# Two transformer blocks in one kernel: order of the opening, of the delta rule's decays and of two smaller steps

## The reference, cut to what matters

```python
h = rmsnorm(x, norm_mix_g);  proj = h @ w_in          # 1024 x 9248: qkv, z, gates ga and gb, ...
qkv = silu(causal_depthwise_conv(concat([gq, gk, gv]), gdn_conv_w))       # 3 x 8 heads x 128
g = -exp(a_log) * softplus(ga + dt_bias);  beta = sigmoid(gb)
# gated delta rule, chunk by chunk; gc = cumsum(g) within a chunk
decay = exp(where(incl, gc[:, None] - gc[None, :], -inf))
lower = where(strict, beta[:, None] * (k @ k.T) * decay, 0)
u, w  = triangular_solve(lower, [beta * v, beta * exp(gc) * k], unit_diagonal=True)
a_qk  = (q @ k.T) * decay
delta = u - w @ state;  o = (q * exp(gc)) @ state + a_qk @ delta
state = exp(gc[-1]) * state + (k * exp(gc[-1] - gc)).T @ delta
o_a = rmsnorm(o) * silu(z)                                     # z: one of w_in's parts
# gated linear attention, 4 heads: scores of decayed q and k, then the same recurrence
# second block: mod = silu(c) @ ada_w + ada_b (for tokens), mod_c the same of c_ctx
```

## Time and profile before

| | us |
|---|---|
| median of three executions | 2690.18 |
| lowest, highest | 2688.42, 2690.37 |
| the profiled execution: time | 2693.22 |
| the profiled execution: span from first to last instruction | 2691.6 |
| busy in it: PE, DVE, ACT, POOL | 2604.5, 1388.5, 908.1, 160.8 |
| granted TensorE clock, mean over the span | 0.987 |

### The profile page before, as it was taken

One profiled execution on the slowest core, in us unless ns is written; L12 is line 12 of the kernel. 1 busy time (PEld: TensorE's weight loads), 2 busy tenths in 40 slices (PEclk: granted clock), 3 DMA queues, 4 the chain that ended last, 5 costly groups with the idle time before them and its releaser, 6 DMA issues.

```text
span 2691.6 us, 34182 instructions
## 1 busy us (share of the span) xinstructions
PE 2604.5 (97%) x14939; PEld 2188.7 (81%) x14939; DVE 1388.5 (52%) x1679; ACT 908.1 (34%) x1254; POOL 160.8 (6%) x177
## 2 busy tenths in 40 slices
PE   6998999999999999999999989899999999999998
PEld 5887888888889788888888977778888788788887
DVE  5665544344466347665565177376643544443334
ACT  4342223343334442222432267332222322322222
POOL 0003110000000010000022000100000100000001
PEclk9999999999999999999999999999999999999999
DMA  3220002221334234563222100166522222222321
GB/s 124 93 79 18 27 8 79 94 79 63 107 112 144 77 125 172 184 210 124 93 87 79 63 1 1 63 221 217 194 103 86 86 98 100 85 94 95 109 91 67
DMA packets 39301, 265.73 MB, mean 99 GB/s; under 512 B 4256, under 2 KB 4640, under 8 KB 8944
## 3 DMA queue, kind: packets, MB, share of 16 engines
q1 hardware_dynamic: 29520, 205.67, 22.1%
q0 software_dynamic: 8256, 55.41, 5.9%
q10 hardware_dynamic: 1376, 2.47, 0.2%
HBM read 261.43 MB, written 2.10 MB: 98 GB/s over the span
## 4 chain that ended last, share of the span: by engine, by line
PE 88%; DVE 7%; ACT 4%; issue 1%; DMA 0%; DVEq 0%; ACTq 0%
PE bank L142 87%; DVE w_lo L151 1%; ACT w_hi L148 1%; PE bank L145 1%; DVE tmp L159 1%; DVE dd L151 1%; ACT da_p L148 1%; DVE da_stat L162 1%; DVE h_lo L159 0%; ACT L148 0%; ACT tmp L148 0%; DVE heads_t L159 0%; ACT da_pt L148 0%; DVE change L151 0%; DVE x_t L159 0%
## 5 line engine op out<-in xcount | busy, mean ns | idle before, releaser
L142 PE MATMUL bank<-h_hi,w_hi 128*128 128x512 f32 (+1 forms) x1992 | 797.7, 400 | 12.8 <-DVE w_lo L151 9.1
L142 PE MATMUL bank<-h_hi,w_lo 128*128 128x512 f32 (+1 forms) x1992 | 780.5, 392 | 0.0
L142 PE MATMUL bank<-h_lo,w_hi 128*128 128x512 f32 (+1 forms) x1992 | 746.2, 392 | 3.9 <-DVE h_lo L151 3.8
L151 DVE TENSOR_TENSOR w_lo<-w_raw,w_hi 128x2048 fp32r<-128x2048 f32 (+2 forms) x197 | 444.9, 2259 | 308.1 <-ACT w_hi L148 308.0
L148 ACT ACTIVATE w_hi<-w_raw 128x2048 fp32r<-128x2048 f32 (+2 forms) x197 | 370.6, 1881 | 311.0 <-PE bank L142 301.2
L142 PEld LDWEIGHTS bank<-h_hi,w_hi 128*128 128x128 f32 (+1 forms) x1992 | 376.0, 189 | 94.7 <-DVE w_lo L151 11.3
L142 PEld LDWEIGHTS bank<-h_lo,w_hi 128*128 128x128 f32 (+1 forms) x1992 | 374.9, 188 | 90.2 <-DVE h_lo L151 10.2
L142 PEld LDWEIGHTS bank<-h_hi,w_lo 128*128 128x128 f32 (+1 forms) x1992 | 376.3, 189 | 74.7 <-issue 1.4
L142 PE MATMUL bank<-f_hi,w_hi 128*128 128x512 f32 x672 | 263.0, 391 | 0.0
L142 PE MATMUL bank<-f_hi,w_lo 128*128 128x512 f32 x672 | 262.4, 390 | 0.0
L142 PE MATMUL bank<-f_lo,w_hi 128*128 128x512 f32 x672 | 248.7, 390 | 0.0
(11 more groups left out here) (332 smaller groups left out, 3241.1 us busy)
## 6 DMA issues: line engine op xcount, KB each, us to landing
w_raw<-in_pack_ffn SPq DMA_DIRECT2D x60, 1024.0 KB, 4.9
ada_w<-in_ada_w POOLq DMA_DIRECT2D x48, 1024.0 KB, 5.3
w_raw<-in_pack_mlp SPq DMA_DIRECT2D x32, 1024.0 KB, 5.1
w_raw<-in_pack_gdn_qkv SPq DMA_DIRECT2D x12, 1024.0 KB, 4.9
w_raw<-in_pack_sc_cu SPq DMA_DIRECT2D x8, 1024.0 KB, 4.9
w_raw<-in_pack_ffn SPq DMA_DIRECT2D x8, 768.0 KB, 4.2
w_raw<-in_pack_gdn_z SPq DMA_DIRECT2D x4, 1024.0 KB, 4.9
w_raw<-in_pack_gate_a SPq DMA_DIRECT2D x4, 1024.0 KB, 5.0
```

What stands on the lines that cost most here:

```text
L142: return self.engine.matmul(*a, **k) if self.engine is not None else self
L151: return self.engine.tensor_tensor(*a) if self.engine is not None else self
```

## The change

1. **Opening.** The parts of `x` are the first DMAs: parts 1 and 3 on ScalarE's queue ahead of `prm`, parts 0 and 2 on SyncE's ahead of panel 0; SyncE holds panel 1 back until part 1 of `x` has landed; `kept_consts` and `scan_consts` go to GpSimd's queue. The waits for constants stand behind the squares. `gates_tensor` does panel 1 (the first two tiles of q) in the same loop over k as the gates; panel 1's hi x lo follows behind the loop, and the splits of panels 1 and 2 move up. TensorE gets five extra matmuls of 384 columns on constants (`warm_up`).
2. **Delta rule.** The decays of chunk c+1 are computed behind level 8 of chunk c, its products k k^T and `low` behind `p64`, its first level behind `change`; those of chunk 0 before z's GEMM. The decays lie in `e_t`, `e_row` for even chunks and in `tmp` for odd ones, decay times beta in `sq`. z's panels are split in four pieces of 512 columns.
3. **Gated linear attention.** A head's scores come one step of the background later (9 yields for 8, and one fewer behind them).
4. **Modulation.** A yield between the sums of `ada_acc` and of `ada_accc`; ScalarE, VectorE and GpSimd have one to match.

```diff
+    def split_hi_piece(S, n, i):
+
+        cut = slice(i * panel_size(n) // PIECES, (i + 1) * panel_size(n) // PIECES)
+        if i == 0:
+            S.wait_ge(*loaded(f"raw_loaded{n % 2}", n // 2 + 1))
+            S.wait_ge(*at("pe_tile", ("panel", n - 2)))
+        S.activation(w_hi[n % 2][:, cut], w_raw[n % 2][:, cut], ACT.Copy).then_inc(
+            *up("act_hi", (n, i), *([n] if i == PIECES - 1 else [])))
...
+    def gemm_beside(lane, split, key, evacuate, block=0, panels=None, token_tiles=0, split_from=0,
+                    piece=None):
 
         for i, nk, width, groups, first in panel_groups(key, block, panels, token_tiles):
-            if split is not None and i >= split_from:
-                split(lane, number[key, block, i] + 1)
+            ahead = number[key, block, i] + 1
+            if split is not None and i >= split_from and piece is None:
+                split(lane, ahead)
+            steps = 0
             for group in groups:
                 for k in range(nk):
+                    if piece is not None and steps < 2 * PIECES and steps % 2 == 0:
+                        piece(lane, ahead, steps // 2)
+                    steps += 1
                     yield
...
+    def load_x(lane, parts):
+        for i in parts:
+            lane.dma_start(x_t[:, 2 * i:2 * i + 2, :], x_in[:, 2 * i:2 * i + 2, :]).then_inc(sems[f"x_loaded{i}"], 16)
+
     def load_scalar(S):
+        load_x(S, (1, 3))
         S.dma_start(prm[:, :], dram["params"]).then_inc(sems["prm_loaded"], 16)
-        S.dma_start(kept_consts[:, :, :], consts_in[:, 0:N_KEPT, :]).then_inc(sems["consts_loaded"], 16)
-        for i in range(DT // 2):
-            S.dma_start(x_t[:, 2 * i:2 * i + 2, :], x_in[:, 2 * i:2 * i + 2, :]).then_inc(sems[f"x_loaded{i}"], 16)
+
+    def load_pool(G):
+        G.dma_start(kept_consts[:, :, :], consts_in[:, 0:N_KEPT, :]).then_inc(sems["consts_loaded"], 16)
+        G.wait_ge(*loaded("x_loaded3"))
+        G.dma_start(scan_consts[:, :, :], consts_in[:, N_KEPT:, :]).then_inc(sems["scan_consts_loaded"], 16)
...
+    def warm_up(T_, rings, name, n):
+
+        bank, before = rings.work.take(("busy", name))
+        T_.wait_ge(*freed(before))
+        T_.wait_ge(*loaded("consts_loaded"))
+        for _ in range(n):
+            done = T_.matmul(bank[:, 0:N_KEPT * P], const("ident"), flat(kept_consts[:, :, :]), start=True, stop=True)
...
+        T_.wait_ge(*at("act_hi", 1))
         for k in range(DT):
             rounded, rest = mix_norm.done(k)
             T_.wait_ge(*rounded)
-            T_.matmul(bank[0:32, :], hi[:, k, :], h_hi[:, k, :], start=(k == 0), stop=False)
-            T_.matmul(bank[0:32, :], lo[:, k, :], h_hi[:, k, :], start=False, stop=False)
+            T_.matmul(g_out, g_hi[:, k, :], h_hi[:, k, :], start=(k == 0), stop=False)
+            T_.matmul(g_out, g_lo[:, k, :], h_hi[:, k, :], start=False, stop=False)
+            for out, cut in q_outs:
+                T_.matmul(out[:, :], q_hi[:, k, cut], h_hi[:, k, :], start=(k == 0), stop=False)
             T_.wait_ge(*rest)
-            done = T_.matmul(bank[0:32, :], hi[:, k, :], h_lo[:, k, :], start=False, stop=(k == DT - 1))
-        done.then_inc(*up("pe_tile", tile, ("panel", 0)))
+            done = T_.matmul(g_out, g_hi[:, k, :], h_lo[:, k, :], start=False, stop=(k == DT - 1))
+            if k == DT - 1:
+                done.then_inc(*up("pe_tile", gates, ("panel", 0)))
+            for out, cut in q_outs:
+                T_.matmul(out[:, :], q_hi[:, k, cut], h_lo[:, k, :], start=False, stop=False)
+        T_.wait_ge(*at("dve_lo", 1))
+        for tile, (out, cut) in zip(queries, q_outs):
+            for k in range(DT):
+                done = T_.matmul(out[:, :], q_lo[:, k, cut], h_hi[:, k, :], start=False, stop=(k == DT - 1))
...
     def gates_scalar(S):
-        split_hi(S, 1)
+        split_hi(S, 2)
...
+    def decays_of(grp, c):
+
+        if c % 2:
+            return four_heads(tmp[grp]), four_heads(tmp[2 + grp])
+        return scan_tiles[grp]["e_t"][:, :, :], scan_tiles[grp]["e_row"][:, :, :]
...
+        def decays(c):
+            bank = bank_for(c, "e_row")
+            four(bank, lambda h: gv[:, c, 4 * grp + h:4 * grp + h + 1].to_broadcast([P, P]),
+                 lambda h: const("incl_t")).then_inc(*up("pe_gdn", (grp, c, "e_row")))
+
+        def products(c):
+            k_of = lambda h: k_t[:, 4 * grp + h, chunk_of(c)]
+            bank = bank_for(c, "low")
+            four(bank, k_of, k_of).then_inc(*up("pe_gdn", (grp, c, "low")))
...
+                if s == 8 and c < NCH - 1:
+                    yield
+                    decays(c + 1)
...
+                yield
+                products(c + 1)
...
     def scan_scalar(S, grp):
...
+        def decays(c):
+            e_t, e_row = (flat(a) for a in decays_of(grp, c))
+            S.wait_ge(*at("dve_gdn", (grp, c, "between")))
+            S.activation(e_t, e_t, ACT.Exp).then_inc(*up("act_gdn", (grp, c, "e_t")))
+            if c >= 2:
+                S.wait_ge(*at("pool_gdn", (grp, c - 2, "q_decayed")))
+                S.wait_ge(*at(state_by(c - 2), (grp, c - 2, "state")))
+            take(c, "e_row", e_row, whole, ACT.Exp)
...
+                if s == 8 and c < NCH - 1:
+                    yield
+                    decays(c + 1)
...
+        def products(c):
+            e_t, _ = decays_of(grp, c)
+            V.wait_ge(*at("act_gdn", (grp, c, "e_t")))
+            V.tensor_tensor(e_beta, e_t, col_of(bv3, c), ALU.mult).then_inc(*up("dve_gdn", (grp, c, "e_beta")))
+            bank = psum(c, "low")
+            V.wait_ge(*at("dve_gdn", (grp, c, "e_beta")))
             if c > 0:
-                V.wait_ge(*at("pe_gdn", (grp, c - 1, "state")))
-            V.tensor_tensor(change[:, :, :], e_t[:, :, :], col_of(bv3, c), ALU.mult).then_inc(
-                *up("dve_gdn", mark("e_beta")))
-            bank = psum(c, "low")
-            V.wait_ge(*at("dve_gdn", mark("e_beta")))
+                V.wait_ge(*at("pool_gdn", (grp, c - 1, f"off{LEVELS[-1]}")))
             for i, half in enumerate(HALVES):
-                V.tensor_tensor(low[half, :, :], change[half, :, half], bank4(bank)[half, :, half], ALU.mult).then_inc(
-                    *up("dve_gdn", mark(f"low{i}")))
-            yield
-            V.wait_ge(*at("dve_gdn", mark("low1")))
+                V.tensor_tensor(low[half, :, :], e_beta[half, :, half], bank4(bank)[half, :, half], ALU.mult).then_inc(
+                    *up("dve_gdn", (grp, c, f"low{i}")))
             if c > 0:
-                V.wait_ge(*at("pe_gdn", (grp, c - 1, "state")))
+                V.wait_ge(*at("pe_gdn", (grp, c - 1, "p64")))
+            V.tensor_tensor(corner[0:HB, :, :], e_beta[0:HB, :, HB:P], bank4(bank)[0:HB, :, HB:P],
+                            ALU.mult).then_inc(*up("dve_gdn", (grp, c, "corner"), frees=(grp, c, "low")))
...
+            if c < NCH - 1:
+                first_level(c + 1)
...
     def scan_with_gate_tensor(T_, rings):
         rings.gemm, wide = rings.few, rings.gemm
         steps = in_turn([scan_tensor(T_, rings, 0), scan_tensor(T_, rings, 1)])
+        for _ in range(4):
+            next(steps)
         drain(beside(z_tensor(T_, rings, "gdn_z"), steps, *SCAN_PACE))
         drain(steps)
...
-            for _ in range(8):
+            for _ in range(9):
                 yield
...
                 done.then_inc(*up("pe_ada", (layer, j, which)))
-            yield
+                yield
...
     def tensor_program(T_):
         rings = Rings()
         Ring.holder.clear()
-        constants_there(T_)
+        warm_up(T_, rings, "sums", 3)
         mix_sum.over_partitions(T_, rings)
         mix_sum.spread(T_, rings)
+        warm_up(T_, rings, "first", 2)
         gates_tensor(T_, rings)
...
+            if n == 0:
+                load_x(Y, (0, 2))
+            elif n == 1:
+                Y.wait_ge(*loaded("x_loaded1"))
+            else:
                 Y.wait_ge(*at("dve_lo", n - 2))
```

More of the change, by code:

```diff
@@ L930, in conv_tensor @@
         T_.background, T_.pace = scan_sums_tensor(T_, rings), 4
-        drain(gemm_tensor(T_, rings, "gdn_qkv", h_done(mix_norm), after=squares))
+        for _ in range(2):
+            T_.step()
+        drain(gemm_tensor(T_, rings, "gdn_qkv", h_done(mix_norm), panels=(1, 12), after=lambda n: squares(n + 2)))
         T_.finish()
@@ L1283, in scan_vector @@
+        products(0)
+        first_level(0)
+        yield
+        for c in range(NCH):
+            mark = lambda name: (grp, c, name)
+            a_t, e_row = decays_of(grp, c)
+            yield
             bank = psum(c, "a_t")
-            V.tensor_tensor(flat(a_t[:, :, :]), flat(e_t[:, :, :]), bank[:, :], ALU.mult).then_inc(
+            V.tensor_tensor(flat(a_t), flat(a_t), bank[:, :], ALU.mult).then_inc(
                 *up("dve_gdn", mark("a_t"), frees=mark("a_t")))
@@ L1389, in scan_pool @@
                     off_level(c, 4 * s)
-            for _ in range(4 + 2 * (c < NCH - 1)):
```

(11 more changed lines are left out.)

148 lines of the change are left out of this document (80 added, 68 removed).

## The result

The changed kernel takes 2669.03 us (median of four, 2667.59 to 2671.17), the kernel before 2690.27: ratio 0.9929, 95% interval 0.9914 to 0.9944. It is 21 us faster; I had forecast 35 (2655). The whole range, 2641 to 2671, just holds it, but my own case's, 2647 to 2661, does not. The direction was right and the size was not.

A forecast was written before the change was run, and what follows sets the result against it. TensorE, busy 2604.5 of 2691.6 us, was taken to bound the kernel, leaving idle time and half clock to gain: opening 8.5, delta rule 15.9, linear attention 7.6, modulation 3.4, sum 35.4; forecast 2655 us, range 2641 to 2671.

The forecast's parts named there:

- my own case: Whole kernel: all four parts gain as summed, 2655 us, range 2647 to 2661, chance 0.6.
- Apart by an output tile, 24 matmuls: Modulation: separating the sums of one column avoids the half clock behind them; gain 3.4 us, from 0 to 3.4.
- 16.7 - 7.6 = 9.1: Delta rule: 16.7 us of TensorE standing still at four chunk starts goes, 7.6 us of new waits come.
- 6.8 and no new fall: Delta rule: 6.8 us of half clock around the chunk starts goes, and the clock is 1.00 there.
- The exponentials' waits: Delta rule, ScalarE: exponentials ahead of level 16's `pp` cost about 2.9 us in chunk 0, 1.45 in chunks 1 and 2.
- The wait for `w_lo`: Z's second panel: VectorE's pieces, behind chunk 0's preparation, come at 16.1 us for TensorE's 14.35; 1.8 us wait.
- rival (a): Delta rule: exponentials on ScalarE's queue hold up both groups by 2 us more, half clock returns; 2665 us, chance 0.2.
- The third scores: Linear attention: one yield more cuts the third head's wait from 3.81 to 1.4 us, without half clock; gain 7.6 us.
- rival (c): Linear attention: the clock still falls behind the wait, 4.6 us come back; 2660 us, chance 0.08.
- issue time alone: Opening: queues share the DMA engines, so `x` comes sooner by 0.93 us and no more; the opening gains about 6.
- the order of bytes: Opening: `x` no longer stands behind panel and constants, all landed at about 8 us; norm 3.5 us sooner.
- K + 17.6: Opening: VectorE ends `w_lo` of panel 3 17.6 us after the gates' loop ends (K, 32.4); a new stall of 2.35.

The follow-up runs named there:

- mod_undone: The changed kernel with the modulation's edit taken back, so the pairs of sums stay together: 2659.75 us, ratio 0.9893 against the kernel before.
- the three repairs: The changed kernel without the modulation's edit, with GpSimd's `q_dec` of chunk 0 at level 16 and the exponentials behind level 16's `pp`: 2656.2 us, ratio 0.9872.

## Why the forecast was 14 us off

**Modulation: the step that failed.** "Apart by an output tile, 24 matmuls ... Gain 3.4, from 0 to 3.4." I asked only what the yield does to the sums, and put what it does to the rest of its background at nothing, without a reason. It also moves all that its generator and the one chained behind it still have to issue, on four engines, against the GEMM. The norm behind the sums lost 6.8 us, half of the 13.4 by which the trace's 22.0 misses my sum: shown by the edit alone (slower than before, with the wait) and by three kernels without the wait. The sums gained 4.7, and 1.7 of this was luck: it came from the second pair, which the edit leaves together and whose half clock cost 1.7 us instead of 3.4. The 3.4 is the whole fall behind the first pair, which some executions don't have (two times of the kernel before, above). And the earlier trace rows show only one of the pair's two sums, so its 2.74 us is not what "sixteen" matmuls took; the pair took 4.4.

**Delta rule: right mechanism, mis-sized terms.** The waits at the chunk starts and the half clock behind them are gone. Over the whole rule, from the first of the seven points to the second (us, TensorE's busy time first), before and after:

```profile
184.23:515.19 330.96, 308.94 (x3452) 266.05 (x3453) 158.17 (x267) 86.65 (x144) 47.41 (x55) 0.97 0.13 43
...
176.78:495.54 318.76, 304.83 (x3452) 263.21 (x3451) 157.22 (x279) 87.23 (x155) 43.16 (x55) 0.98 0.13 44
```

TensorE stood still for 22.0 us before and 13.9 after, a gain of 8.1 where I had 16.7 - 7.6 = 9.1. Half clock, by its overlap with busy time, cost 8.6 before and 4.6 after, a gain of 4.1 where I had 6.8 and no new fall. The exponentials' waits were forecast at 5.8 and are 2.51, 1.00 and 0.81. The wait for `w_lo` was forecast at 1.8 and is 4.97, 2.1 of it through the two pieces that ran beside GpSimd's `q_dec`: I took every piece as a quarter of 2.29 us. Of the remaining 1 us half is the first piece's 1.21 beside `off`; the rest has no experiment. Behind the two longest new waits the clock fell, 2.9 and 1.7 us. That is rival (a) in part: the second of these waits, 2.51 us, was shorter than the 2.9 that I had spoken of against it.

**Linear attention.** The third scores wait 1.23 us where I had 1.4:

```profile
581.30 0.44 PE L142 MATMUL bank<-gla_qin,gla_kin 128*64 128x64 f32 x2 [1.23 <-ACT heads_t L148]
```

The waits came out as forecast, but 5.8 us were gained and not 7.6. Behind this wait the changed kernel has 1.5 us of half clock left of the 4.6, which looks like a third of rival (c). It is not the reason. In the 14 traces with this edit the stretch from the second point to the third takes 139.58 to 139.67 us. In four of them the clock fell behind the wait; in the other ten, `mod_undone` among them, it did not, and there TensorE waited for VectorE 29 us later instead:

```profile
609.93 1.13 PE L142 MATMUL bank<-gla_at,gla_v 128*128 128x128 f32 x8 [1.75 <-DVE gla_at L151]
```

Where the clock fell this wait is 0.4 to 0.5 us. So the step that failed is that every microsecond taken away at the third scores was counted as gained: the next thing that TensorE needs, `gla_at`, was not ready sooner, a wait that the forecast put at nothing.

**Opening.** The changed kernel's timeline, beside the earlier trace rows:

```profile
0.74 1.02 ACTq L180 DMA_DIRECT2D x_t<-in_x_t  x2
...
7.45 2.29 DVE L151 TENSOR_TENSOR rstd<-rstd,sq 128x512 f32<-128x512 f32 x3 [7.45 <-ACT sq L148]
10.28 3.08 DVE L151 TENSOR_TENSOR rstd<-rstd,sq 128x512 f32<-128x512 f32 x4 [0.53 <-ACT sq L148]
...
18.12 1.41 DVE L159 SCALAR_TENSOR_TENSOR tmp<-x_t,prm,bank 128x512 f32<-128x512 f32 x2 [2.24 <-PE bank L142]
```

The adds begin at 7.45, where I had 6.5, and pause once for `x`; the norm begins at 18.12 for 16.65, 2.0 us sooner than before instead of 3.5. That is more than issue time alone (0.93) and less than I took from the order of bytes; parts went to a second queue as well, and no run here tells the two apart. Panel 3's last `conv_in` begins at 63.42 for 70.90, 7.5 us sooner and 1 us under the forecast. My working has a slip of the same size: K + 17.6 and the panel's 10.9 are K + 28.5, not 29.5. Over all traces the last `conv_in` lies at 181.4 to 184.2 with the old opening (four) and at 174.6 to 176.8 with the new (13), 7.2 us between the means.

## What to carry to other kernels

A yield in a paced background is an edit of everything that is issued behind it: follow the background to its end, in the trace, and give the yield back where something is idle. Read a duration that two engines may share from a row in which both are busy. Where a wait is shortened, look for the next one behind it before the whole is counted as gained. And a fall of the clock avoided is worth little as a forecast: behind the same instructions it came in one kernel and not in another, and one kernel's executions take two times that differ in granted clock.

## What the runs showed of the hardware

- VectorE's subtraction on 128x512 took 0.68 us with GpSimd idle, 1.21 beside GpSimd's `off` and 1.75 beside its `q_dec` (changed kernel, and the same with `q_dec` late).
- The clock's fall is not a property of the instructions ahead of it: the same pair of sums was followed by 3.4, 1.7 or 0 us of loss in kernels that differ only in other parts, and the differential attention, unchanged in all kernels, lost 5.9 us in one trace and 3.4 in another.
- Behind the same wait of 1.23 us the clock fell in four of 14 traces, at a loss of 1.5 to 1.7 us, and did not in ten.
- One kernel's executions can lie at two times: 2684 or 2691 us for the kernel before, at a granted clock of 0.991 or 0.988; 2653 or 2660 for the one with the three repairs, at 0.996 or 0.992 to 0.993.
